# Scores' second products on 64 rows each, with a second copy of the rounded queries

## The chip, the cores and the metric

One core of a Trainium2 chip runs the program. The metric is the device time of one execution in microseconds (us). A row of matmul on TensorE is called PE, a load of its stationary operand (weights) PEld, VectorE is DVE, ScalarE is ACT, GpSimd is POOL, and the DMA queue of SyncE is SPq.

## What is computed

One encoder layer on two sequences (512 and 1024 tokens, width 1024). The change touches the scores of the attention heads:

```python
q = proj[..., :ATTN_WIDTH].reshape(B, S, N_Q_HEADS, HEAD_DIM)      # 8 heads of 64
k = proj[..., ATTN_WIDTH:ATTN_WIDTH + KV_WIDTH].reshape(B, S, N_KV_HEADS, HEAD_DIM)   # 2 heads of 64
...
s = jnp.einsum('bqkgd,bskd->bkgqs', qi, k, preferred_element_type=jnp.float32) * scale
p = jax.nn.softmax(s, axis=-1).astype(v.dtype)
return jnp.einsum('bkgqs,bskd->bqkgd', p, v)
```

Around it stand a norm, an input projection, a pooling mixer, an output projection and a squared-ReLU MLP of width 4096.

## The kernel before

Every matrix product keeps float32 accuracy with operands in a rounded format (fp32r). A value x is split into a high part (x rounded) and a low part (x minus the high part), and the products high x high, low x high and high x low are summed in PSUM.

**The scores.** A head is 64 deep and the array has 128 rows. So the tile `Qs` (line 126) holds, for each query block, the rounded queries on 64 partitions and their low parts on the other 64. `KA` holds the rounded keys on both halves of the partitions, `KB` the keys' low parts on both halves. One product of `Qs` with `KA` thus gives high x high plus low x high, and one of `Qs` with `KB` gives high x low plus low x low (line 1072). `scores(s, pair, idx, u)` makes one *unit*: two outputs of 128x512 (`h` = 0 and 1) in two neighbouring PSUM banks. For each `h` it issues the product with `KA` and then the one with `KB`. `s.n` is 0 for the short sequence (the prompt) and 1 for the long one (the sample). In a prompt unit the two outputs are two blocks of 128 queries against all 512 keys; in a sample unit they are one block of queries against the two halves of the keys.

**The jobs.** A job is 4 units. The prompt has 4 jobs (`pair` 0 to 3, two heads each), the sample 16 (`pair` 0 to 3, `idx` 0 to 3: one head of the pair and one half of its queries). A job has 8 turns `k`. In a turn TensorE transposes four 128x128 blocks of the exponentials `prob` two turns ahead (L1088) and multiplies the turn's transposed block by the values (`values`, L1103 with the high part `pThi`, L1104 with the low part `pTlo`). In every odd turn it also makes one unit of scores of a later job (`scored_in`): in turn 1 the last unit of the next job, in turns 3, 5 and 7 the first three of the job after it. Three PSUM banks hold the transposes, four the units, one the sum over the values.

**What the other engines do for a job.** ACT rounds each transposed block (`pThi`, L1339), makes the exponentials (L1424), and copies the result out (`o_full`). DVE subtracts (`pTlo`, L1837), takes the maxima of each unit (L1899), and for the sample copies value tiles for the next heads (`Vg`, L2022, two copies in four jobs). Between PE, ACT and DVE there are semaphores only: PE's `values` waits for `pTlo`, a unit of scores waits for the exponentials of the unit that had its banks (`exp_done`). The order on each engine is that of the code.

**The split of the queries.** For the prompt ACT rounds the queries (`split_q`, line 1400, eight calls, the last four of them beside the attention itself) and DVE or POOL makes the low parts. For the sample POOL does both (`split_q`, line 2506), three jobs ahead: rounding (L2516), then the low part (L2519). POOL also adds and scales the outputs (L2537, L2543) and computes the pooling windows.

The sample's pairs 0 to 2 are a loop (`Fori`) on PE, ACT and DVE; the last pair is written out.

Of the kernel before, what the change touches and what calls it, by code (L numbers as in the profile page):

```python
# [7 lines left out]
ALU = mybir.AluOpType  # L8
# [3 lines left out]
F32R = mybir.dt.float32r  # L12

P = 128
# [3 lines left out]
NQ, NKV = 8, 2  # L18
# [9 lines left out]
TT = T // P  # L28
# [23 lines left out]
def hybrid_layer(nc, x, g1, w_in, gqk, w_pool, pool_scale, w_out, g2, w_up, w_down,  # L52
                 ident_d, rope_d, edge_d, y):
    with ExitStack() as ctx:
        def sem(name):
            return ctx.enter_context(nc.semaphore(name))

        def at(name, off, shape, dt=F32):
            return nc.alloc_sbuf_tensor_at(name, [P] + shape, dt, offset=BASE + off)
# [42 lines left out]
        S = R + 43008  # L102
# [12 lines left out]
        KA = [at("KA0", X + 20480, [NKV, SEQ_P], F32R), at("KA1", S + 6144, [NKV, SEQ_S], F32R)]  # L115
        KB = [at("KB0", W, [NKV, SEQ_P], F32R), at("KB1", S + 14336, [NKV, SEQ_S], F32R)]
        Qs = at("Qs", W + 4096, [4, 512], F32R)
# [4 lines left out]
        o_full = at("o_full", S, [2, 512])  # L122
        o_part = at("o_part", S + 4096, [512])
        rinvb = at("rinvb", S + 32768, [512])
        rinvb_last = at("rinvb_last", R + 38912, [512])
        rinvd = nc.dram_tensor("rinvd", [3 * NQ, P, 4], F32).ap()
        sw_sample = [at(f"sw_sample{i}", S + 22528 + i * 4160, [SEQ_S + 2 * PAD]) for i in range(2)]
# [77 lines left out]
        ps = ctx.enter_context(nc.psum_tensor("ps", [P, 8, 512], F32))  # L205
# [29 lines left out]
        u_done = sem("u_done")  # L235
# [107 lines left out]
        FIRST = 1  # L343
# [45 lines left out]
        def pair_kv(pair):  # L389
            return pair // (NQ // 2 // NKV)  # L390
# [50 lines left out]
        def qk_cols(a, j, c0, n):  # L441
            return QT[a:a + 64, c0 // 32:(c0 + n) // 32, bass.ds(j, 1), :].rearrange("p b a t -> p b (a t)")

        def blocks(cols):
            return cols.rearrange("p (b t) -> p b t", t=32)
# [490 lines left out]
        def _(pe):  # L936
# [115 lines left out]
            def scores(s, pair, idx, u):  # L1052
                g = s.group(pair, idx, u)
                half = u // 2 if s.n == 0 else 0
                if u % (GRP // s.halves) == 0:
                    pe.wait_ge(q_lo[s.n], s.out(pair, idx, half) - NQ * s.n + 1)
                pe.wait_ge(k_dup[0], 32 + 32 * s.n)
                if s.n == 0:
                    pe.wait_ge(k_dup[1], 32)

                if not isinstance(g, int) or g >= 2:
                    pe.wait_ge(exp_done, g - 1)
                kv = pair_kv(pair)
                for h in range(2):

                    qt = u if s.n else 2 * (u % 2) + h
                    key0 = h * 512 * s.n
                    out = ps[:, 2 * (u % 2) + h]
                    q = Qs[:, 2 * s.parity(pair, idx) + half, qt * P:(qt + 1) * P]
                    pe.matmul(out, q, KA[s.n][:, bass.ds(kv, 1), key0:key0 + 512].rearrange("p a c -> p (a c)"),  # L1070
                              start=True, stop=False)
                    mm = pe.matmul(out, q, KB[s.n][:, bass.ds(kv, 1), key0:key0 + 512].rearrange("p a c -> p (a c)"),  # L1072
                                   start=False, stop=True)
                mm.then_inc(s_done, 1)

# [54 lines left out]
            def attend(s, pair, last=False):  # L1130
                for idx in range(s.per):
                    if s.n and idx == 3:
                        pe.wait_ge(k_dup[1], 64)
                    for k in range(STEPS):
                        if transposed_in(s, pair, idx, k) and not (s.n == 0 and pair == 0 and k == 0):
                            transpose_p(*transposed_in(s, pair, idx, k))


                        ends = (k + 1) % s.kts == 0
                        if ends:  # L1140
                            values(s, pair, idx, k)
                        if scored_in(s, pair, idx, k):
                            scores(*scored_in(s, pair, idx, k))
                        if not ends:
                            values(s, pair, idx, k)
                        if last and (idx, k) == (2, 3):
                            turn_wp()
                        if last and (idx, k) in FOLDS:
                            fold(FOLDS.index((idx, k)))

            def first_scores(u):

                if u == 0:

                    pe.wait_ge(qk_copied, FIRST + TT - 1)
                    pe.wait_ge(v_lo, FIRST + TT - 1)
                if u == 1:

                    pe.wait_ge(qk_copied, FIRST + TT)
                    pe.wait_ge(v_lo, FIRST + TT)  # L1160
                scores(seqs[0], 0, 0, u)
# [12 lines left out]
            project_block(NB - 1, True)  # L1174

            scores(seqs[0], 1, 0, 0)

            pe.wait_ge(u_saved, FIRST + TT // 2)
# [4 lines left out]
            scores(seqs[0], 1, 0, 2)  # L1183
            for pair in range(NQ // 2):
                attend(seqs[0], pair)
            with pe.Fori(0, NQ // 2 - 1) as pair:
                attend(seqs[1], pair)
            attend(seqs[1], NQ // 2 - 1, True)

# [142 lines left out]
        def _(act):  # L1332
# [5 lines left out]
            def copy(out, in_, **kw):  # L1338
                return act.activation(out, in_, ACT.Copy, **kw)  # L1339
# [59 lines left out]
            def split_q(s, pair, idx, unit):  # L1399

                j = s.job(pair, idx)
                act.wait_ge(qT_in[s.n], 16 * s.len // P)
                half = s.half_of(idx, unit * s.kts)
                a, c0 = half * 64, s.start + idx // 2 * 512

                if not isinstance(j, int) or j >= 2:
                    act.wait_ge(s_done, GRP * (j - 1))
                if isinstance(j, int) and j == 0 and unit == 0:

                    act.wait_ge(hT_lo, TT)  # L1410
                copy(blocks(Qs[a:a + 64, 2 * s.parity(pair, idx) + unit]), qk_cols(a, pair, c0, 512)).then_inc(q_hi, 1)

            def exps(s, pair, idx, u):
# [42 lines left out]
            def project_block(n, last):  # L1456
                for i in range(2 if n == 0 else 0, 4):
                    t = n * 4 + i
                    copy_qkv(t, qkv_banks(i))
                    square_qk(t)  # L1460
                    if t + 2 < TT:

                        act.wait_ge(u_done, FIRST + t // 2)
                        split_hT(t + 2, (i + 2) % 4)
                        square_x(t + 2)
                    if last and i == 1:

                        split_k(0, 0)
                        split_k(0, 1)
                        for pair in range(2):  # L1470
                            for unit in range(2):
                                split_q(seqs[0], pair, 0, unit)
                    if last and i == 3:

                        act.wait_ge(u_done, FIRST + TT // 2 - 1)
                        exps(seqs[0], 0, 0, 0)
                        exps(seqs[0], 0, 0, 1)
                    if last and i == 3:
                        exps(seqs[0], 0, 0, 2)
                        exps(seqs[0], 0, 0, 3)  # L1480
# [931 lines left out]
        def _(pool):  # L2412
# [93 lines left out]
            def split_q(s, pair, idx):  # L2506

                a, b = idx % 2 * 64, (1 - idx % 2) * 64
                c0, m = s.start + idx // 2 * 512, s.out(pair, idx, 0) - NQ + 1

                if done:
                    pool.wait_ge(win_step, done)
                pool.wait_ge(qT_in[s.n], 16 * s.len // P)
                pool.wait_ge(s_done, GRP * (s.job(pair, idx) - 1))
                pool.wait_ge(q_hi, NQ + m - 1)
                pool.tensor_scalar(blocks(Qs[a:a + 64, 2 * (idx % 2)]), qk_cols(a, pair, c0, 512), 1.0, 1.0, ALU.mult, ALU.mult  # L2516
                                   ).then_inc(q_hi, 1)
                pool.wait_ge(q_hi, NQ + m)
                pool.tensor_tensor(blocks(Qs[b:b + 64, 2 * (idx % 2)]), qk_cols(a, pair, c0, 512),  # L2519
                                   blocks(Qs[a:a + 64, 2 * (idx % 2)].bitcast(F32)), ALU.subtract).then_inc(q_lo[1], 1)  # L2520
                pool.wait_ge(q_lo[1], m)
# [67 lines left out]
            for s in seqs:  # L2589
                for pair in range(NQ // 2):  # L2590
                    for idx in range(s.per):
# [6 lines left out]
                        if nxt3 and nxt3[0].n:  # L2598
                            split_q(*nxt3)
# [155 lines left out]
```

## Time and profile before

| | |
|---|---|
| median of 3 runs | 1474.98 us (1473.99 to 1475.79) |
| profiled execution, its own time | 1475.89 us |
| its span in the trace | 1474.1 us |
| granted TensorE clock, mean | 0.999 |
| units of scores | 80 (16 prompt, 64 sample), 160 products with `KA`, 160 with `KB` |

The page gives the busy time of each engine, the span in 40 slices of 36.9 us, the chain of work that ended last and the costliest groups of instructions. A matmul's row has a modelled end: its duration is longer than the distance to the next matmul's start, so that the cost of a matmul is read from the distance of two starts.

### The profile page before, as it was taken

How to read it: one execution, taken by the hardware profiler on the slowest of the kernel's cores; microseconds unless marked ns; L12 is line 12 of the kernel's file. 1: busy time of each engine (PE TensorE's matmuls, PEld its weight loads, DVE VectorE, ACT ScalarE, POOL GpSimd, SP SyncE). 2: the span in 40 equal slices, each digit the busy share in tenths (PEclk: the TensorE clock that was granted, in tenths of full speed). 3: DMA queues.
4: the chain of work that ended last, by engine and by line, in shares of the span. 5: the costliest groups of instructions: out<-in, count | busy, mean ns of one | idle time of the engine just before them, and what ended most of it. 6: DMA issues, size and time to landing. Idle time of an engine off the chain costs nothing.

```text
span 1474.1 us, 23234 instructions
## 1 busy us (share of the span) xinstructions
PE 1463.4 (99%) x7812; PEld 1306.9 (89%) x7812; DVE 1055.7 (72%) x1254; ACT 729.1 (49%) x1251; POOL 398.1 (27%) x363
## 2 busy tenths in 40 slices
PE   9999999999999999999999999999999999999999
PEld 8999878888888889999999999999888888888887
DVE  6765799999868785544454454449887888878875
ACT  6232398888847755545555554546322322323220
POOL 3457567666745420000000000001220211311300
PEclk9999999999999999999999999999999999999999
DMA  8644341111245849333233334347644344343434
GB/s 263 149 119 118 82 126 34 40 25 24 81 164 192 292 154 380 128 144 141 103 143 133 136 114 151 121 174 278 253 157 158 100 157 126 117 155 109 138 97 183
DMA packets 94443, 212.30 MB, mean 144 GB/s; under 512 B 12080, under 2 KB 31408, under 8 KB 94256
## 3 DMA queue, kind: packets, MB, share of 16 engines
q1 hardware_dynamic: 92192, 200.46, 40.8%
q10 hardware_dynamic: 2192, 11.08, 1.8%
q8 instruction: 33, 0.54, 0.2%
q14 instruction: 26, 0.21, 0.1%
HBM read 133.08 MB, written 71.62 MB: 139 GB/s over the span
## 4 chain that ended last, share of the span: by engine, by line
PE 97%; ACT 1%; DVE 1%; issue 1%; DMA 0%; POOL 0%; ACTq 0%; SPq 0%; DVEq 0%; POOLq 0%
PE ps L943 24%; PE ps L944 24%; PE ps L945 24%; PE ps L1206 6%; PE ps L1088 4%; PE ps L1216 3%; PE ps L1103 2%; PE ps L1070 2%; PE ps L1104 2%; PE ps L1072 2%; ACT prob L1424 0%; DMA ident<-in_ident 0%; ACT pThi L1339 0%; PE ps L968 0%; PE ps L972 0%
## 5 line engine op out<-in xcount | busy, mean ns | idle before, releaser
L943 PE MATMUL ps<-h,wuhi 128*128 128x384 f32 (+1 forms) x904 | 301.5, 333 | 0.2 <-issue 0.2
L944 PE MATMUL ps<-h,wuhi 128*128 128x384 f32 (+1 forms) x904 | 301.1, 333 | 0.0
L945 PE MATMUL ps<-h,wulo 128*128 128x384 f32 (+1 forms) x904 | 301.1, 333 | 0.0
L943 PE MATMUL ps<-wdhi,hidhi 128*128 128x512 f32 x672 | 261.6, 389 | 0.0
L945 PE MATMUL ps<-wdhi,hidlo 128*128 128x512 f32 x672 | 261.5, 389 | 0.0
L944 PE MATMUL ps<-wdlo,hidhi 128*128 128x512 f32 x672 | 261.5, 389 | 0.0
L2328 DVE TENSOR_TENSOR yacc<-yacc,ps 128x1024 f32<-128x1024 f32 x167 | 203.1, 1216 | 78.8 <-PE ps L945 78.8
L1339 ACT ACTIVATE hidhi<-hin 128x1024 fp32r<-128x1024 f32 (+1 forms) x72 | 86.8, 1205 | 301.0 <-PE ps L945 291.8
L2242 DVE TENSOR_TENSOR u<-u,ps 128x384 f32<-128x384 f32 x96 | 53.0, 553 | 181.6 <-PE ps L945 181.6
L943 PEld LDWEIGHTS ps<-h,wuhi 128*128 128x128 f32 x904 | 169.7, 188 | 0.7 <-issue 0.4
L944 PEld LDWEIGHTS ps<-h,wuhi 128*128 128x128 f32 x904 | 169.7, 188 | 0.0
L945 PEld LDWEIGHTS ps<-h,wulo 128*128 128x128 f32 x904 | 169.7, 188 | 0.0
L943 PEld LDWEIGHTS ps<-wdhi,hidhi 128*128 128x128 f32 x672 | 126.1, 188 | 26.8 <-issue 0.4
L944 PEld LDWEIGHTS ps<-wdlo,hidhi 128*128 128x128 f32 x672 | 126.1, 188 | 26.1
L945 PEld LDWEIGHTS ps<-wdhi,hidlo 128*128 128x128 f32 x672 | 126.1, 188 | 26.1
L2684 POOL TENSOR_TENSOR hout<-h,hout 128x384 f32<-128x384 f32 x1 | 1.7, 1748 | 477.3 <-PE ps L945 477.3
L1837 DVE TENSOR_TENSOR pTlo<-ps,pThi 128x512 fp32r<-128x512 f32 x160 | 107.9, 686 | 12.4 <-ACT pThi L1339 9.6
L1837 DVE TENSOR_TENSOR hidlo<-hin,hidhi 128x1024 fp32r<-128x1024 f32 (+1 forms) x72 | 111.5, 1549 | 5.4 <-ACT hidhi L1339 5.4
L1643 ACT ACTIVATE hout<-u 128x384 f32<-128x384 f32 x96 | 50.4, 525 | 124.8 <-DVE u L2242 113.5
L1339 ACT ACTIVATE pThi<-ps 128x512 fp32r<-128x512 f32 x160 | 95.0, 601 | 26.4 <-PE ps L1088 19.7
L1088 PEld LDWEIGHTS ps<-ident,prob 128*128 128x128 f32 x640 | 79.3, 140 | 22.7 <-DVE pTlo L1837 1.4
L1424 ACT ACTIVATE prob<-ps,nmax 128x1024 f32<-128x1024 f32 (+1 forms) x96 | 93.0, 974 | 11.5 <-DVE nmax L1899 11.3
(229 smaller groups left out, 2813.8 us busy)
## 6 DMA issues: line engine op xcount, KB each, us to landing
hd<-hout SPq DMA_DIRECT2D x64, 384.0 KB, 3.2
hin<-hd SPq DMA_DIRECT2D x48, 512.0 KB, 3.6
hd<-hout SPq DMA_DIRECT2D x32, 576.0 KB, 2.8
hin<-hd SPq DMA_DIRECT2D x24, 768.0 KB, 4.4
wuraw<-in_w_up SPq DMA_DIRECT2D x17, 1024.0 KB, 5.9
wdraw<-in_w_down SPq DMA_DIRECT2D x8, 2048.0 KB, 9.3
h<-h2d ACTq DMA_DIRECT2D x7, 1536.0 KB, 10.8
x2in<-in_x SPq DMA_DIRECT2D x12, 512.0 KB, 3.3
```

The lines of the kernel that those rows point to most:

```text
L943: pe.matmul(out, w_hi, m_hi, start=start, stop=False, skip_group_check=resumed)
L944: pe.matmul(out, w_hi, m_lo, start=False, stop=False, skip_group_check=resumed)
L945: return pe.matmul(out, w_lo, m_hi, start=False, stop=stop, skip_group_check=resumed)
L1088: mm = pe.transpose(ps[:, 4 + k % 3, qt * P:(qt + 1) * P], prob[s.parity(pair, idx)][:, u, c0:c0 + P], ident[:])
L1206: pe.matmul(ps[:, 2 * i + h], c[i][:, k], wohi[:, j, h * 512:(h + 1) * 512], start=(j == 0 and c is chi), stop=False)
L1216: mm = pe.matmul(ps[:, 2 * i + h], chi[i][:, SLOT_ROWS[j]], wolo[:, j, h * 512:(h + 1) * 512], start=False, stop=(n == KT - 1))
L1339: return act.activation(out, in_, ACT.Copy, **kw)
L1424: ins = act.activation(prob[b][:, u, c0:c0 + s.len], psw[:, (u % 2) * 1024 + c0:(u % 2) * 1024 + c0 + s.len], ACT.Exp, bias=nmax[:, b, q:q ...
L1643: act.activation(out, src, ACT.Relu).then_inc(relu_done, 1)
L1837: return dve.tensor_tensor(out, a, b.bitcast(F32), ALU.subtract)
L2242: dve.tensor_tensor(u, u, up_bank(par, (1, 4, 5)[k]), ALU.add).then_inc(u_sum, 1)
L2328: dve.tensor_tensor(q, q, down_banks(u, o), ALU.add).then_inc(acc_done, 1)
```

## The change

The two products with `KA` come first, then the two with `KB`. For 72 of the 80 units (all but those of prompt pairs 0 and 1) each of the two products with `KB` uses only 64 rows: output 0 partitions 0 to 63, output 1 partitions 64 to 127, each with the rounded queries alone, so that the product low x low is no longer in the sum. The array is addressed as a tile of 64 rows for each of them (rows 0 to 63, rows 64 to 127). Since `Qs` has the rounded queries on one half of the partitions only, a new tile `Qh` holds them on the other half. ACT fills it for prompt pairs 2 and 3 (one more copy ahead of that of `Qs`, and a wait for the end of the input projection, whose weights lay there), POOL for every sample job. PE's loop over the sample's pairs 0 to 2 is written out (512 more matmuls in the program, as many as before executed).

```diff
+        Qh = at("Qh", S + 34816, [2, 512], F32R)
@@ scores
                 for h in range(2):
-                    q = Qs[:, 2 * s.parity(pair, idx) + half, qt * P:(qt + 1) * P]
-                    pe.matmul(out, q, KA[s.n][:, bass.ds(kv, 1), key0:key0 + 512].rearrange("p a c -> p (a c)"),
+                    c, keys, out = part(h)
+                    pe.matmul(out, Qs[:, 2 * slot + half, c], KA[s.n][:, bass.ds(kv, 1), keys].rearrange("p a c -> p (a c)"),
                               start=True, stop=False)
-                    mm = pe.matmul(out, q, KB[s.n][:, bass.ds(kv, 1), key0:key0 + 512].rearrange("p a c -> p (a c)"),
+                for h in range(2):
+                    c, keys, out = part(h)
+                    if s.n == 0 and pair < 2:
+                        r = slice(0, P)
+                    else:
+                        r = slice(h * 64, h * 64 + 64)
+                    q = Qh[r, slot, c] if r.stop - r.start == 64 and h != high else Qs[r, 2 * slot + half, c]
+                    mm = pe.matmul(out, q, KB[s.n][r, bass.ds(kv, 1), keys].rearrange("p a c -> p (a c)"),
                                    start=False, stop=True)
@@ TensorE's stream
-            with pe.Fori(0, NQ // 2 - 1) as pair:
+            for pair in range(NQ // 2 - 1):
                 attend(seqs[1], pair)
@@ ScalarE's split_q
+                if s.n == 0 and pair >= 2:
+                    act.wait_ge(u_done, FIRST + TT // 2)
+                    copy(blocks(Qh[64 - a:128 - a, s.parity(pair, idx)]), qk_cols(a, pair, c0, 512))
@@ GpSimd's split_q
+                pool.tensor_scalar(blocks(Qh[b:b + 64, idx % 2]), qk_cols(a, pair, c0, 512), 1.0, 1.0, ALU.mult, ALU.mult)
```

On PE, in the first job of the sample, turns 0 to 3, before (`prob_96` is the job's buffer of exponentials; the ISA and REGISTER_ALU rows are the loop's registers):

```order
L1088 MATMUL ps<-ident,prob_96 128x128 x4
L1062 ISA
L1070 ISA
L1070 MATMUL ps<-KA_92,Qs 128x512
L1072 REGISTER_ALU
L1072 MATMUL ps<-KB_94,Qs 128x512
L1070 ISA
L1070 MATMUL ps<-KA_92,Qs 128x512
L1072 REGISTER_ALU
L1072 MATMUL ps<-KB_94,Qs 128x512
L1101 REGISTER_ALU
L1103 MATMUL ps<-pThi,Vg 128x512
```

The same place now:

```order
L1099 MATMUL ps<-ident,prob_96 128x128 x4
L1074 MATMUL ps<-KA_92,Qs 128x512 x2
L1083 MATMUL ps<-KB_94,Qh 128x512
L1083 MATMUL ps<-KB_94,Qs 128x512
L1114 MATMUL ps<-pThi,Vg 128x512
L1115 MATMUL ps<-pTlo,Vg 128x512
```

The two products with the low parts are neighbours, between the two with the rounded keys and the values or the next transposes; the register instructions are gone.

On ACT, in the prompt's pair 0, where it rounds the queries of pairs 2 and 3, before:

```order
L1339 ACTIVATE pThi<-ps 128x512
L1339 ACTIVATE Qs<-QT 64x512
L1339 ACTIVATE pThi<-ps 128x512
L1424 ACTIVATE prob_96,rsum<-ps,nmax 128x512 x2
L1339 ACTIVATE Qs<-QT 64x512
L1339 ACTIVATE pThi<-ps 128x512 x2
```

The same place now:

```order
L1350 ACTIVATE pThi<-ps 128x512
L1350 ACTIVATE Qh<-QT 64x512
L1350 ACTIVATE Qs<-QT 64x512
L1350 ACTIVATE pThi<-ps 128x512
L1438 ACTIVATE prob_96,rsum<-ps,nmax 128x512 x2
L1350 ACTIVATE Qh<-QT 64x512
L1350 ACTIVATE Qs<-QT 64x512
L1350 ACTIVATE pThi<-ps 128x512 x2
```

Each copy into `Qs` has one into `Qh` ahead of it, and the next `pThi` comes behind both. POOL's stream has the same pattern, one `Qh` ahead of each `Qs` in the sixteen sample jobs.

## Rows read from the trace of the kernel before

**Rows 1.** The page, parts 1 and 2: busy time, granted clock in 40 slices.

```profile
PE 1463.4 (99%) x7812; PEld 1306.9 (89%) x7812; DVE 1055.7 (72%) x1254; ACT 729.1 (49%) x1251; POOL 398.1 (27%) x363
...
PEclk9999999999999999999999999999999999999999
```

**Rows 2.** Busy time by stretch: PE, PEld, DVE, ACT, POOL (instructions), clock, DMA.

```profile
190.00:217.00 27.00, 26.05 (x144) 20.43 (x144) 25.13 (x37) 25.73 (x63) 17.89 (x15) 1.00 0.40 114
217.00:237.00 20.00, 19.94 (x117) 16.48 (x116) 19.20 (x25) 18.14 (x37) 15.39 (x13) 1.00 0.23 48
240.00:393.00 153.00, 152.08 (x893) 127.48 (x891) 144.82 (x190) 133.51 (x237) 104.79 (x84) 1.00 0.13 28
```

**Rows 3.** DVE's waits from 240 to 393 us: total, times, longest.

```profile
DVE pTlo L1837 <- ACT pThi L1339: 5.1, 26, 0.2
```

**Rows 4.** Timeline of PE in sample jobs: start, duration, operation.

```profile
302.47 0.60 PE L1088 MATMUL ps<-ident,prob 128*128 128x128 f32 x4
302.82 0.48 PE L1070 MATMUL ps<-KA,Qs 128*128 x1
303.14 0.39 PE L1072 MATMUL ps<-KB,Qs 128*128 x1
303.14 0.19 PEld L1070 LDWEIGHTS ps<-KA,Qs 128*128 128x128 f32 x1
303.37 0.40 PE L1070 MATMUL ps<-KA,Qs 128*128 x1
...
303.60 0.40 PE L1072 MATMUL ps<-KB,Qs 128*128 x1
303.84 0.39 PE L1103 MATMUL ps<-pThi,Vg 128*128 128x512 f32 x1
...
304.65 0.48 PE L1103 MATMUL ps<-pThi,Vg 128*128 128x512 f32 x1
...
315.55 0.48 PE L1103 MATMUL ps<-pThi,Vg 128*128 128x512 f32 x1
```

**Rows 5.** Timeline of DVE in a stretch without idle time, prompt.

```profile
191.28 1.28 DVE L1837 TENSOR_TENSOR pTlo<-ps,pThi 128x512 fp32r<-128x512 f32 x2
192.47 0.17 DVE L1909 RECIPROCAL rinv<-rsum 128x4 f32<-128x4 f32 x1
...
193.13 1.21 DVE L1899 TENSOR_REDUCE nmax<-ps 128x2 f32<-128x1024 f32 x1
194.26 1.28 DVE L1837 TENSOR_TENSOR pTlo<-ps,pThi 128x512 fp32r<-128x512 f32 x2
```

**Rows 6.** Timeline of ACT around its roundings of the prompt's queries.

```profile
185.88 0.63 ACT L1339 ACTIVATE Qs<-QT 64x512 fp32r<-64x512 f32 x1
187.34 0.69 ACT L1424 ACTIVATE prob<-ps,nmax 128x512 f32<-128x512 f32 x1 [0.83 <-DVE nmax L1899]
...
199.67 0.63 ACT L1339 ACTIVATE Qs<-QT 64x512 fp32r<-64x512 f32 x1
200.19 1.07 ACT L1339 ACTIVATE pThi<-ps 128x512 fp32r<-128x512 f32 x2
...
204.05 0.63 ACT L1339 ACTIVATE Qs<-QT 64x512 fp32r<-64x512 f32 x1
204.70 0.69 ACT L1424 ACTIVATE prob<-ps,nmax 128x512 f32<-128x512 f32 x1
```

**Rows 7.** Timeline of POOL in a sample job.

```profile
303.93 1.29 POOL L2537 TENSOR_TENSOR attc<-o_full,o_part 64x512 f32<-64x512 f32 x1 [3.84 <-DMA o_part<-o_full]
...
306.95 0.61 POOL L2516 TENSOR_SCALAR Qs<-QT 64x512 fp32r<-64x512 f32 x1
```

**Rows 8.** Timeline where PE waits in the sample: DVE and PE.

```profile
365.46 2.32 DVE L2022 CAST Vg<-V 128x512 fp32r x1
...
368.52 0.47 PE L1103 MATMUL ps<-pThi,Vg 128*128 128x512 f32 x1 [0.92 <-DVE pTlo L1837]
```

More of the change, by code:

```diff
@@ L1063, in scores, with part @@
                 kv = pair_kv(pair)
-                for h in range(2):
-                    qt = u if s.n else 2 * (u % 2) + h
-                    key0 = h * 512 * s.n
-                    out = ps[:, 2 * (u % 2) + h]
-                    q = Qs[:, 2 * s.parity(pair, idx) + half, qt * P:(qt + 1) * P]
-                    pe.matmul(out, q, KA[s.n][:, bass.ds(kv, 1), key0:key0 + 512].rearrange("p a c -> p (a c)"),
-                              start=True, stop=False)
-                    mm = pe.matmul(out, q, KB[s.n][:, bass.ds(kv, 1), key0:key0 + 512].rearrange("p a c -> p (a c)"),
+                slot = s.parity(pair, idx)
+                high = idx % 2 if s.n else half
+                def part(h):
+                    qt = u if s.n else 2 * (u % 2) + h
+                    return slice(qt * P, (qt + 1) * P), slice(h * 512 * s.n, h * 512 * s.n + 512), ps[:, 2 * (u % 2) + h]
+                for h in range(2):
+                    c, keys, out = part(h)
+                    pe.matmul(out, Qs[:, 2 * slot + half, c], KA[s.n][:, bass.ds(kv, 1), keys].rearrange("p a c -> p (a c)"),
+                              start=True, stop=False)
+                for h in range(2):
[6 more added lines that the diff above has]
+                    mm = pe.matmul(out, q, KB[s.n][r, bass.ds(kv, 1), keys].rearrange("p a c -> p (a c)"),
                                    start=False, stop=True)
```

## The prediction

> **What bounds the kernel now.** I read the page first. TensorE is busy 99% of the span at the full granted clock [rows 1], so what an edit gives or costs on TensorE is the first question, and where another engine is nearly as full is the second. So I cut the attention into stretches [rows 2]. From 240 to 393 us (the sample jobs that still score) PE is busy 152.08 of 153 us, DVE 144.82 and ACT 133.51. There PE waits once, 0.92 us, behind a long `Vg` copy on DVE [rows 8]. DVE waits 5.1 us in all, in 26 short waits for ACT [rows 3], which itself follows PE's transposes. PE therefore sets the pace of the sample, with DVE some 5% behind it. From 190 to 217 us (prompt pairs 0 and 1) it is another picture: ACT is busy 25.73 of 27 us, more than DVE (25.13), and PE's modelled durations hide that it is not tight. From 217 to 237 us PE leads again (19.94 of 20), with ACT at 18.14 and DVE at 19.20.
>
> The timeline gives the unit costs [rows 4]. The start of one 128x512 product lies 0.23 us from the next (303.14, 303.37, 303.60, 303.84). The first product behind the transposes takes 0.32 (302.82 to 303.14), so a weight load that nothing hides costs about 0.09. Four transposes take 0.35. One job lasts 315.55 - 304.65 = 10.90 us.
>
> **The change part by part.**
>
> *The `KB` products.* A unit takes 4 x 0.23 = 0.92 us (1.01 behind transposes). If the two products on 64 rows run side by side, one 0.23 goes: that is the upper bound of the gain for a unit. If they run one behind the other, nothing goes. Against it stand two changes of the array's tiling in each unit, into 64 rows and back to 128, which the trace of before does not contain. Bounds for one of them from the nearest rows: nothing, if it is hidden like the steps at 303.37 and 303.60; 0.09 us if only a weight load comes to the open, as behind the transposes; 0.39 - 0.23 = 0.16 us if the next product has to wait for the modelled end of the last one; 0.16 + 0.09 = 0.25 us if both come together. So a unit changes by -0.23 + 2 x (0 to 0.25), from -0.23 to +0.27 us. The step behind the transposes is the nearest row, since it too is a change of what the array does. There it appears on one side only (the step into the transposes takes the usual 0.23), so I take 0.08 us in all for a unit and a net of -0.15 us.
>
> At this place the Trainium skill speaks on both sides. The page TensorEngine Tiling (Array Packing), section Tiling Modes, says that changing the tiling mode drains TensorE; by that rule each of the two changes costs at least the 0.16, a unit comes out 0.09 us longer, and the sum turns positive (the rival *full drain* below). The page TensorE: Matmul & The Clock Gate, Part 3, estimates the span of several row tiles as one matmul plus about 4 ns for each further tile, which gives the full 0.23 and says nothing of mixing them with full-height products. No row here can decide between them.
>
> *How many units count.* 57 units are scored inside sample jobs (the last of job 1, and four each of jobs 2 to 15), where PE leads: 57 x 0.15 = 8.6 us. DVE caps this. It has 153 - 144.82 = 8.2 us idle there [rows 2], and when its operations follow without idle time they overlap: the maxima take 1.13 instead of 1.21 (193.13 to 194.26), and two `pTlo` 1.19 instead of 1.28 [rows 5]. With 56 maxima this frees another 4.5 us, so DVE could follow by up to 12.7. The 8.6 fits, but the two `Vg` copies of each four jobs already push PE into a wait once, and with a faster PE they will do so more often. I take 7.5 of the 8.6.
>
> The other 15 tiled units are scored in the prompt. Eight or so lie before 217 us, where ACT is full: nothing. Seven lie in the stretch at 217 to 237 us: 7 x 0.15 = 1.1, of which half, since ACT and DVE have only 1.9 and 0.8 us of idle time there. That is 0.6.
>
> *ACT's four copies into `Qh`.* The first comes at 185.9, where ACT waits 0.83 us right behind (until 187.34) [rows 6]; one more copy at 0.55 is hidden, and the added wait for the end of the projection is past by then, since the maxima of the next unit wait for it as well. The other three lie in pair 0 and at the start of pair 1, where ACT is full. The step of such a copy is 0.52 (199.67 to 200.19) to 0.65 us (204.05 to 204.70); I take 0.55 each, 1.65 us, all on the path, because the next `pThi` and exponentials stand behind them and PE waits for those. Below it could be 0 if a later wait swallows it.
>
> *POOL's sixteen copies.* Each takes 0.61 us [rows 7]. In a sample job POOL waits 3.84 us for a DMA at the place shown, and it splits the queries of a job more than one job before PE asks for them. The cover is that lead; without it a job would lose 0.61. I take nothing.
>
> *The written-out loop.* PE has no idle time at the loop's turns now, so nothing is to be won; the register instructions sit between products that start 0.23 apart as anywhere. More program has to be fetched, as in the prompt, which is written out and shows no hole that recurs. I take nothing.
>
> **The sum.** -7.5 - 0.6 + 1.65 = -6.45 us against the profiled execution's 1475.89 (its span 1474.1, 1.8 around it), so 1469.4. That execution lies 0.9 above the median of the runs; against 1474.98 the forecast is **1468.5 us**.
>
> **The rivals.** 0.2% of this time is 2.95 us, about what a measurement can tell from no change.
>
> - *Side by side and cheap* (the forecast; a unit gains 0.12 to 0.23 us): 1463 to 1471 us. For it: weight loads start together with the product before them, on the same 128 rows (the load and the product at 303.14 [rows 4]), so loads for a 64-row tile should be hidden too. Chance 0.40.
> - *The changes of tiling eat the gain* (0.09 each, a unit gains 0.05): 57 x 0.05 = 2.9, less 1.65, so 1473.7; with the neighbouring values 1472 to 1477. Chance 0.19.
> - *Full drain, slower.* The place is each unit's two borders. The point from which it decides is 0.11 us for one change of tiling, above which a unit gets longer. At 0.16 each it costs 0.09 x 72 = 6.5, and with ACT's 1.65, less what is hidden in the prompt, 1482; at 0.25 each it costs 0.27 x 57 = 15.4, some 2 in the prompt and 1.65, so 1494. For it: a modelled duration of 0.39 against 0.23 shows work still in the array when the next product starts, and a change of its shape may have to wait for that. Against it: the transposes are a change of mode too and cost 0.09 only. Chance 0.29, of which 0.10 beyond 1488.
> - *No overlap at all* (two 64-row products one behind the other, no price for the change): only ACT's copies are left, 1476.6. Chance 0.05.
> - *DVE becomes the bound at once*: its waits for ACT (5.1 us) turn out to be latency that stays, so that it gives back only 3 of 8.2 us: 1475 - 3 + 1.65 = 1473.6. Chance 0.07.
>
> **How the numbers follow.** Faster by over 0.2%: the first case and a little of the second, 0.43. Within 0.2%: most of the second, the fourth and the fifth, 0.27. Slower: 0.30. The range 1462 to 1488 leaves out only the heavy drain; the forecast's own range is 1463 to 1471.
>
> **What the profile after would show.** If right, the second of the two `KB` products starts less than 0.1 us behind the first, the `KA` product before and the values behind it start at 0.23 to 0.3 us, and a sample job takes about 10.3 us instead of 10.90, with DVE close to full. Pairs 0 and 1 are longer by 1 to 2 us, from ACT. If the drain rules, the first `KB` product starts 0.35 us or more behind the `KA` one, and what stands behind the second too, with a job above 10.9. If the starts of the two `KB` products lie 0.23 apart, they do not overlap. What would make the prediction wrong is above all the price of the two changes of tiling, which enters 57 times.

## The result, and the profile after

The changed kernel takes **1485.78 us** (median of 6 runs, 1485.21 to 1487.92) against 1474.80 of the kernel before on the same chip (6 runs, 1473.99 to 1475.79): ratio 1.008, 95% interval 1.007 to 1.009. It is slower by 11.0 us. The forecast was 1468.5. What came is the rival *full drain*. One run in all is left out of a median here, one of e10, which took 2341.02 us at a mean clock of 0.567.

The page of the changed kernel, parts 1 and 2 (beside [rows 1]):

```profile
PE 1473.1 (99%) x7812; PEld 1286.3 (87%) x7812; DVE 1059.3 (71%) x1254; ACT 732.0 (49%) x1255; POOL 407.6 (27%) x379
...
PEclk9999999999999999999999999999999999999999
```

The same number of matmuls at the same clock keeps PE busy for 9.7 us longer (1463.4 before), although pairs of them now run at the same time. The clock is out of the question.

Busy time by stretch of the changed kernel (columns as in [rows 2]):

```profile
190.00:217.00 27.00, 24.75 (x131) 16.12 (x130) 23.18 (x35) 25.53 (x60) 16.26 (x15) 1.00 0.40 104
217.00:237.00 20.00, 20.00 (x112) 14.20 (x112) 18.74 (x25) 17.48 (x36) 16.16 (x15) 1.00 0.23 48
240.00:393.00 153.00, 152.19 (x846) 106.74 (x845) 138.90 (x179) 126.25 (x225) 105.17 (x92) 1.00 0.13 28
```

From 240 to 393 us PE is as busy as before, but gets through 846 matmuls instead of 893, 5% fewer. DVE does 179 operations instead of 190, and is busy 138.90 us instead of 144.82. So PE still sets the pace, and it is a slower pace. From 190 to 217 us ACT is the full engine, as before.

The timeline of PE in the sample jobs, as [rows 4] (start, duration, operation; a row with x2 or x4 holds that many neighbours):

```profile
301.81 0.60 PE L1099 MATMUL ps<-ident,prob 128*128 128x128 f32 x4
302.17 0.70 PE L1074 MATMUL ps<-KA,Qs 128*128 128x512 f32 x2
302.80 0.49 PE L1083 MATMUL ps<-KB,Qh 64*128 64x512 f32 x1
302.80 0.49 PE L1083 MATMUL ps<-KB,Qs 64*128 64x512 f32 x1
303.22 0.50 PE L1114 MATMUL ps<-pThi,Vg 128*128 128x512 f32 x1
303.56 0.39 PE L1115 MATMUL ps<-pTlo,Vg 128*128 128x512 f32 x1
...
304.15 0.48 PE L1114 MATMUL ps<-pThi,Vg 128*128 128x512 f32 x1
...
315.66 0.47 PE L1114 MATMUL ps<-pThi,Vg 128*128 128x512 f32 x1
```

The two `KB` products have the same start, 302.80: they run side by side, and one step of 0.23 us is gone. Around them every step is longer. From the first `KA` product to the first `KB` one it is 0.63, where 0.32 (behind the transposes) and 0.23 would be 0.55: +0.08. From the pair to the values it is 0.42 instead of 0.23: +0.19. From the first product of the values to the second it is 0.34 instead of 0.23: +0.11. Together that is 0.38 us for the two changes of tiling. The stretch from the first `KA` product to the second product of the values is 303.56 - 302.17 = 1.39 us, against 304.06 - 302.82 = 1.24 before: +0.15 a unit, which is 0.38 - 0.23. The job takes 315.66 - 304.15 = 11.51 us instead of 10.90: +0.61, four units of 0.153.

The weight loads of the same place, PEld:

```profile
302.14 0.30 PEld L1074 LDWEIGHTS ps<-KA,Qs 128*128 128x128 f32 x2
302.79 0.18 PEld L1083 LDWEIGHTS ps<-KB,Qh 64*128 64x128 f32 x1 [0.35 <-issue]
302.80 0.18 PEld L1083 LDWEIGHTS ps<-KB,Qs 64*128 64x128 f32 x1
303.22 0.19 PEld L1114 LDWEIGHTS ps<-pThi,Vg 128*128 128x128 f32 x1 [0.24 <-issue]
```

Before, a load started together with the product before its own (303.14 in [rows 4]). Here the first load after each change starts together with its own product: nothing was fetched across the change. The load path is idle ahead of it, and no semaphore is named, only "issue". In the list of waits from 240 to 393 us PEld has these entries (total us, times, longest), where before it had one, 1.1 us, once, at L1103:

```profile
PEld ps L1083 <- issue: 18.8, 52, 0.4
PEld ps L1114 <- issue: 7.3, 27, 1.0
PEld ps L1099 <- issue: 3.2, 13, 0.2
PEld ps L1114 <- DVE pTlo L1851: 3.2, 13, 0.2
```

The 52 at L1083 are the changes into 64 rows. The others are the 52 changes back, each with 0.24 or 0.25 us: 26 + 13 ahead of the values, 13 ahead of the next transposes (the 27th at L1114, 1.0 us, is the wait behind the long `Vg` copy, as before). For 13 of them DVE is named, at the same length.

**Where the 11 us lie.** I take three marks: the prompt's first product with the values, the sample's first one, and the transposes of `wp_raw`, which PE makes in the sample's last job but one (394.50 us before, 404.57 now). The first two bound "the prompt's stretch", the last two "the sample's". Against the experiment with 128-row products and all copies (e2 below), the prompt's stretch is 49.55 instead of 48.49 us, +1.06, which is the seven tiled units that lie there where PE leads (7 x 0.153 = 1.07). The sample's is 166.72 us against 158.03 before, +8.7: 57 units of 0.153. ACT's copies add 1.8 (e2). That is 11.6 us, for 11.0 measured.

Against e2 the sample's stretch is longer still, 166.72 instead of 157.04, +9.7. The 1.0 above the 57 units lies in a single job, which takes 12.59 us where its neighbours take 11.52. The kernel before has such a job too (12.07 instead of 10.90), and e2 has none. It holds the long `Vg` copy on DVE of [rows 8], for which PE waits 0.81 us in the changed kernel (the last section).

### The profile page after: what moved, and what is told of

Read it like the earlier page. It is cut to its first block, busy times and chain, and to the rows that moved or that the text cites. A ratio compares the mean times of both kernels' runs of the same rounds, so it can differ in the third digit from the quotient of the medians.

```text
span 1484.2 us, 23088 instructions
## 1 busy us (share of the span) xinstructions
PE 1473.1 (99%) x7812; PEld 1286.3 (87%) x7812; DVE 1059.3 (71%) x1254; ACT 732.0 (49%) x1255; POOL 407.6 (27%) x379
## 4 chain that ended last, share of the span: by engine, by line
PE 89%; POOL 4%; issue 2%; ACT 2%; DVE 2%; DMA 0%; ACTq 0%; POOLq 0%; SPq 0%; DVEq 0%
PE ps L944 22%; PE ps L945 22%; PE ps L946 22%; PE ps L1217 6%; PE ps L1099 4%; PE ps L1227 3%; PE ps L1114 3%; PE ps L1115 2%; PE ps L1074 2%; PE ps L1083 2%; POOL rsqk L2440 1%; POOL qsin L2499 1%; POOL sw_prompt L2469 1%; ACT prob L1438 1%; DVE roped L1957 0%
## 5 line engine op out<-in xcount | busy, mean ns | idle before, releaser
L1099 PE MATMUL ps<-ident,prob 128*128 128x128 f32 x640 | 97.1, 274 | 1.1 <-DVE pTlo L1851 0.9
```

The lines of the kernel that those rows point to most:

```text
L1099: mm = pe.transpose(ps[:, 4 + k % 3, qt * P:(qt + 1) * P], prob[s.parity(pair, idx)][:, u, c0:c0 + P], ident[:])
```

## The experiments

In all of them the kernel before ran on the same chip beside the new one. "Step" is the distance between two starts.

### e1_order: the order and the written-out loop alone

The whole change without the 64-row tiles and without `Qh`: the two `KA` products first, 128 rows everywhere.

```diff
-                    if s.n == 0 and pair < 2:
+                    if True:
                         r = slice(0, P)
...
-                    copy(blocks(Qh[64 - a:128 - a, s.parity(pair, idx)]), qk_cols(a, pair, c0, 512))
...
-                pool.tensor_scalar(blocks(Qh[b:b + 64, idx % 2]), qk_cols(a, pair, c0, 512), 1.0, 1.0, ALU.mult, ALU.mult)
```

> The changed kernel with all products on 128 rows and without the copies into Qh: what is left of the change is the order of the four products of a unit and the written-out loop. If the price is the array's change of tiling: no change from before, 1474 to 1476.5 us. If the written-out loop or the order costs: up to the 1486 of the changed kernel.

Measured: 1474.56 us against 1474.43, ratio 0.9999 (0.9990 to 1.0008). Order and loop cost nothing, as the prediction took.

### e2_copies: the copies without the tiles

e1 with ACT's four and POOL's sixteen copies back: only the `if True:` above.

> As the run with order and loop alone, but with ACT's four and POOL's sixteen copies into Qh, which nothing reads. If the tiling is the price: the 1.65 us of the prediction for ACT's copies, so 1475.5 to 1477.5. If the copies are the cause (ACT full in the prompt, POOL late in the sample): 1483 to 1486.

Measured: 1475.02 us, ratio 1.0006 (0.9997 to 1.0015), just below the expected 1475.5 to 1477.5. In the whole time the copies cannot be told from nothing. In the trace they can: the prompt's stretch is 48.49 us instead of 46.72 in e1, +1.77. PE waits for ACT there, in the timeline of PE in e2:

```profile
201.11 0.50 PE L1114 MATMUL ps<-pThi,V 128*128 128x512 f32 x1 [0.91 <-ACT o_full L1350]
```

The changed kernel's timeline has the same wait:

```profile
201.45 0.50 PE L1114 MATMUL ps<-pThi,V 128*128 128x512 f32 x1 [0.79 <-ACT o_full L1350]
```

The sample's stretch, though, is 157.04 us instead of 158.55: 1.5 us come back. They lie in two of its jobs: the one with the long copy takes 10.90 us instead of 12.07, and the first 11.06 instead of 11.41 (the last section has the cause).

### e3_same_tile: both products on rows 0 to 63

The same work, the same two changes of tiling, but no chance to run side by side. Output 1 takes the queries and keys of the lower half here.

```diff
-                        r = slice(h * 64, h * 64 + 64)
-                    q = Qh[r, slot, c] if r.stop - r.start == 64 and h != high else Qs[r, 2 * slot + half, c]
+                        r = slice(0, 64)
+                    q = Qh[r, slot, c] if r.stop - r.start == 64 and high else Qs[r, 2 * slot + half, c]
```

> The changed kernel with both products with KB on rows 0 to 63, so that they can't run side by side; the changes of tiling are as many as in the changed kernel. If the two products do overlap now and the borders are the price: 0.23 us more for each of 72 units, of which 57 on the path, so 1498 to 1503. If they gain nothing from being side by side: 1486.

Measured: 1500.85 us against 1474.43, ratio 1.0179 (1.0163 to 1.0194), 15 us above the changed kernel and inside the expected 1498 to 1503. Without the overlap a unit costs 0.39 more than before (0.153 + 0.24; a sample job takes 12.43 us), and 64 x 0.39 + 1.8 = 26.8 us for the 26.4 measured. The timeline of PE in e3:

```profile
302.87 0.73 PE L1083 MATMUL ps<-KB,Qs 64*128 64x512 f32 x2
303.53 0.50 PE L1114 MATMUL ps<-pThi,Vg 128*128 128x512 f32 x1
303.87 0.39 PE L1115 MATMUL ps<-pTlo,Vg 128*128 128x512 f32 x1
```

From the first `KB` product to the values it takes 0.66 us, in the changed kernel 0.42. The overlap is real and worth 0.24. The step behind it is 0.34 in both. So the pair does what it should, and the loss is around it.

### e4_kb_first: the pair next to the transposes

The `KB` pair ahead of the two `KA` products. If the price were the weight load in the open, which the transposes leave there anyway, the two could share it.

```diff
                 for h in range(2):
-                    pe.matmul(out, Qs[:, 2 * slot + half, c], KA[s.n][:, bass.ds(kv, 1), keys].rearrange("p a c -> p (a c)"),
-                              start=True, stop=False)
+                    pe.matmul(out, q, KB[s.n][r, bass.ds(kv, 1), keys].rearrange("p a c -> p (a c)"),
+                                   start=True, stop=False)
                 for h in range(2):
-                    mm = pe.matmul(out, q, KB[s.n][r, bass.ds(kv, 1), keys].rearrange("p a c -> p (a c)"),
-                                   start=False, stop=True)
+                    mm = pe.matmul(out, Qs[:, 2 * slot + half, c], KA[s.n][:, bass.ds(kv, 1), keys].rearrange("p a c -> p (a c)"),
+                              start=False, stop=True)
```

> The changed kernel with the two 64-row products ahead of the two with KA in each unit, so that the step into 64 rows stands behind the transposes in three of four units, where a weight load is in the open anyway. If the price of a border is in part that load: up to 0.09 us less in 43 units, 1481 to 1484. If it is a drain that comes whatever stands ahead: 1485 to 1487.

Measured: 1486.65 us against 1474.43, ratio 1.0089 (1.0075 to 1.0103): as slow as the changed kernel. The expected 1481 to 1484 of a shared load did not come, and the other outcome did, 1485 to 1487. The timeline of PE:

```profile
302.13 0.60 PE L1099 MATMUL ps<-ident,prob 128*128 128x128 f32 x4
302.66 0.50 PE L1079 MATMUL ps<-KB,Qh 64*128 64x512 f32 x1
302.66 0.50 PE L1079 MATMUL ps<-KB,Qs 64*128 64x512 f32 x1
303.09 0.73 PE L1083 MATMUL ps<-KA,Qs 128*128 128x512 f32 x2
303.66 0.40 PE L1114 MATMUL ps<-pThi,Vg 128*128 128x512 f32 x1
```

The transposes now take 0.53 us to the next start instead of 0.35, the pair 0.43, and the first `KA` product 0.34 (303.66 less the usual 0.23 lies 0.34 behind 303.09). It is the same price in other places: from the transposes to the values 303.66 - 302.13 = 1.53 us, against 303.84 - 302.47 = 1.37 before, +0.16 a unit.

### e5_half and e6_sample: fewer units

e5 tiles prompt pairs 2 and 3 and every second unit of the sample; e6 tiles the sample alone and has no copies on ACT.

```diff
-                    if s.n == 0 and pair < 2:
+                    if s.n == 0 and pair < 2 or s.n and u % 2:
```

```diff
-                    if s.n == 0 and pair < 2:
+                    if s.n == 0:
...
-                    copy(blocks(Qh[64 - a:128 - a, s.parity(pair, idx)]), qk_cols(a, pair, c0, 512))
```

> The changed kernel with 64-row products only in the sample units with even u (32 of 64), and in the prompt as changed. The price goes by units: a job of the changed kernel is 0.61 us longer for four units, so 0.15 for each; 29 fewer such units on the path take back about 4.4 us of the 11.4, 1480 to 1482. If a fixed part (copies, program) carried it: 1484 or more.

> The changed kernel with 64-row products in the sample alone, and without ACT's copies: 64 units tiled. If the sample's units carry the loss (57 x 0.15 = 8.7, and up to 1 for the seven scored late in the prompt): 1483 to 1485. If the prompt's part with ACT's copies is large (2 us or more): 1482 or less.

Measured: e5 1479.64 us against 1473.56, ratio 1.0045 (1.0031 to 1.0059), +6.1, just below the expected 1480 to 1482; e6 1484.96, ratio 1.0078 (1.0064 to 1.0092), +11.4, inside the expected 1483 to 1485. The loss grows with the number of tiled units of the sample: none in e2, 32 in e5, 64 in e6. A sample job of four units takes 10.90 us with none tiled, 11.20 with two (e5) and 11.52 with four (e6). In e6 the sample's stretch is 166.72 us, as in the changed kernel. The whole loss of e6 is 1.6 us above 64 x 0.153 = 9.8. The two stretches account for 10.3 of it (48.02 and 166.72 us, against 46.42 and 158.03 before), and I have no cause for the rest; differences of 1 us between such variants are not resolved by this sum.

### e7_twice and e8_four: the price by itself

e7 makes the `KB` pair twice in a row (so the low parts are counted twice, in the two prompt pairs at 128 rows as well): twice the work on 64 rows, still two changes. e8 goes back to the order `KA`, `KB`, `KA`, `KB` with `KB` on 64 rows: the same work as the changed kernel, four changes, no pair.

```diff
+                    pe.matmul(out, q, KB[s.n][r, bass.ds(kv, 1), keys].rearrange("p a c -> p (a c)"),
+                                   start=False, stop=False)
+                for h in range(2):
...
                     mm = pe.matmul(out, q, KB[s.n][r, bass.ds(kv, 1), keys].rearrange("p a c -> p (a c)"),
                                    start=False, stop=True)
```

```diff
                               start=True, stop=False)
-                for h in range(2):
-                    c, keys, out = part(h)
                     if s.n == 0 and pair < 2:
```

> The changed kernel with the pair of 64-row products made twice in each unit (the prompt pairs 0 and 1 make the full-height ones twice), so the keys' low parts count double. The changes of tiling stay as many. If only the borders are dear and a second pair inside costs one product's step: 0.23 us for 80 units, 65 to 80 of them on the path, 1500 to 1505. If each pair inside 64 rows also costs a weight load in the open (0.32): 1507 to 1512.

> The changed kernel with the four products of a unit in the order of before (KA, KB, KA, KB), the KB ones on 64 rows: four changes of tiling in a unit where there were two, and no two products side by side. With 0.20 us for a change: 4 x 0.20 = 0.80 for each of 72 units, 57 or more on the path, 1520 to 1533. If what costs is something once per unit: 0.23 more than the changed kernel, 1499 to 1503.

Measured: e7 1504.27 us against 1473.56, ratio 1.0208 (1.0193 to 1.0224); e8 1529.05, ratio 1.0374 (1.0358 to 1.0390), +55.5 us, of which 64 x 0.79 + 1.8 = 52.4 come out of the steps below. Both are inside what was expected of a price per change (1500 to 1505, 1520 to 1533). The timeline of PE in e7:

```profile
293.32 0.49 PE L1083 MATMUL ps<-KB,Qh 64*128 64x512 f32 x1
...
293.65 0.39 PE L1092 MATMUL ps<-KB,Qh 64*128 64x512 f32 x1
293.65 0.39 PE L1092 MATMUL ps<-KB,Qs 64*128 64x512 f32 x1
293.98 0.50 PE L1123 MATMUL ps<-pThi,Vg 128*128 128x512 f32 x1
```

From the first pair to the values it is now 0.33 + 0.33 = 0.66 instead of 0.42: a second pair costs 0.24, the price of one ordinary product. The price is per change and not per product. And in e8:

```profile
292.08 0.48 PE L1074 MATMUL ps<-KA,Qs 128*128 128x512 f32 x1
292.49 0.49 PE L1081 MATMUL ps<-KB,Qh 64*128 64x512 f32 x1
292.91 0.50 PE L1074 MATMUL ps<-KA,Qs 128*128 128x512 f32 x1
293.34 0.50 PE L1081 MATMUL ps<-KB,Qs 64*128 64x512 f32 x1
293.77 0.50 PE L1112 MATMUL ps<-pThi,Vg 128*128 128x512 f32 x1
294.11 0.39 PE L1113 MATMUL ps<-pTlo,Vg 128*128 128x512 f32 x1
```

The five steps are 0.41, 0.42, 0.43, 0.43 and 0.34, together 2.03 us. With 128 rows they were 0.32 + 4 x 0.23 = 1.24. Four changes cost 0.79, 0.20 each; a sample job takes 14.02 us instead of 10.90. The steps can also be read as one price in two parts. The first step has only the change ahead of it: 0.41 - 0.32 = 0.09. The last has only the change behind it: 0.34 - 0.23 = 0.11. Those in the middle have both: 0.42 to 0.43 - 0.23 = 0.19 to 0.20. So a change of tiling delays its own product by 0.09 and the next one by 0.11 us. The same two numbers give the steps of e7, 0.23 + 0.11 behind the first pair and 0.23 + 0.09 ahead of the values, for 0.33 and 0.33 measured. The loads of e8:

```profile
292.49 0.18 PEld L1081 LDWEIGHTS ps<-KB,Qh 64*128 64x128 f32 x1 [0.24 <-issue]
292.91 0.19 PEld L1074 LDWEIGHTS ps<-KA,Qs 128*128 128x128 f32 x1 [0.24 <-issue]
293.34 0.18 PEld L1081 LDWEIGHTS ps<-KB,Qs 64*128 64x128 f32 x1 [0.24 <-issue]
```

Each load stands at the start of its own product, with the load path idle ahead of it for 0.24 us and no semaphore named.

### e9_all64: two pairs for one visit

The `KA` products go on 64 rows too, with the rounded queries alone, so the product of the low queries with the rounded keys is left out in the 72 units. Four products on 64 rows then follow each other.

```diff
-                    pe.matmul(out, Qs[:, 2 * slot + half, c], KA[s.n][:, bass.ds(kv, 1), keys].rearrange("p a c -> p (a c)"),
-                              start=True, stop=False)
...
+                    pe.matmul(out, q, KA[s.n][r, bass.ds(kv, 1), keys].rearrange("p a c -> p (a c)"),
+                                   start=True, stop=False)
```

> The changed kernel with the products with KA on 64 rows too, with the rounded queries alone; it leaves out the product of the queries' low parts with the rounded keys in 72 units. A unit is now two pairs side by side between the same two changes of tiling. If those two cost 0.40 us and each pair saves 0.23: 0.46 - 0.40, so 0.06 less than before for each of 57 units and more, 1470 to 1473. If products on 64 rows are slow in themselves: not below the changed kernel's 1485.

Measured: 1471.69 us against 1474.62, ratio 0.9981 (0.9972 to 0.9990), inside the expected 1470 to 1473. Its timeline of PE:

```profile
290.00 0.60 PE L1104 MATMUL ps<-ident,prob 128*128 128x128 f32 x4
290.53 0.50 PE L1079 MATMUL ps<-KA,Qs 64*128 64x512 f32 x1
...
290.87 0.39 PE L1088 MATMUL ps<-KB,Qs 64*128 64x512 f32 x1
...
291.20 0.50 PE L1119 MATMUL ps<-pThi,Vg 128*128 128x512 f32 x1
291.53 0.40 PE L1120 MATMUL ps<-pTlo,Vg 128*128 128x512 f32 x1
```

From the transposes to the second product of the values it is 1.53 us, against 304.06 - 302.47 = 1.59 before: two pairs save 0.46 and two changes cost 0.40. In the whole time this stands beside ACT's copies and the long copy, which is missing here as in e2. Against e2, which has the same copies, the sample's stretch is 153.33 instead of 157.04 us: 57 x 0.065.

### e10_no_low: how far DVE lets PE run

e1 without any `KB` product: the low parts of the keys are left out everywhere. It asks what a much cheaper unit could have brought at most.

```diff
-                    pe.matmul(out, Qs[:, 2 * slot + half, c], KA[s.n][:, bass.ds(kv, 1), keys].rearrange("p a c -> p (a c)"),
-                              start=True, stop=False)
-                for h in range(2):
...
-                    mm = pe.matmul(out, q, KB[s.n][r, bass.ds(kv, 1), keys].rearrange("p a c -> p (a c)"),
-                                   start=False, stop=True)
+                    mm = pe.matmul(out, Qs[:, 2 * slot + half, c], KA[s.n][:, bass.ds(kv, 1), keys].rearrange("p a c -> p (a c)"),
+                              start=True, stop=True)
```

> The kernel with order and loop alone, without any product with KB (the keys' low parts are left out of the scores): TensorE has 0.46 us less in each unit, 1.84 in a job of 10.90. It asks how much a faster TensorE could give at all. If DVE and ACT cap it at 8.2 to 12.7 us of idle time as in the prediction: 1460 to 1467. If they follow with TensorE: 14 jobs x 1.84 = 26 less, 1446 to 1450.

Measured: 1459.87 us against 1474.62, ratio 0.9896 (0.9878 to 0.9914), -14.75 us, at the edge of the expected 1460 to 1467. By PE's steps 0.46 x 57 = 26 us would have gone in the sample alone. Its busy time from 240 to 380 us, columns as in [rows 2]:

```profile
240.00:380.00 140.00, 134.73 (x785) 106.20 (x783) 136.28 (x189) 129.52 (x238) 103.28 (x82) 1.00 0.15 31
```

From the list of PE's waits in the same stretch (total, times, longest):

```profile
PE ps L1090 <- DVE pTlo L1839: 3.0, 14, 0.3
```

DVE is now the fullest engine, at 136.28 of 140 us, and PE waits for its `pTlo` ahead of the transposes in 14 places. Its shortest jobs take 9.8 us, where 10.90 less PE's 1.84 would be 9.06.

### e11_pool: the version to keep

128-row products in the new order, POOL's copies kept, ACT's taken out (e2 showed that these cost 1.8 us in the prompt while something gave 1.5 back in the sample).

```diff
-                    if s.n == 0 and pair < 2:
+                    if True:
...
-                    copy(blocks(Qh[64 - a:128 - a, s.parity(pair, idx)]), qk_cols(a, pair, c0, 512))
```

> All products on 128 rows, order and loop of the changed kernel, POOL's sixteen copies into Qh kept, ACT's four left out. The trace with all the copies was 1.8 us longer in the prompt than the one without any, and 1.5 us shorter in the sample, where the last long Vg copy on DVE took 0.50 us instead of 2.31. If ACT's copies made the first and POOL's shift the second: about 1.5 us less than order and loop alone, 1472.5 to 1473.8, with no Vg copy over 2 us and the prompt stretch (first product with the values to the sample's first) back at 46.7 us. If the two belong together: 1474 to 1475.5.

Measured: 1472.78 us (11 runs) against 1474.27 (15 runs), ratio 0.9989 (0.9980 to 0.9998): 1.5 us faster than the kernel before, and some 13 us faster than the changed one, each set against the runs of before on its own chip (1.008 - 0.9989 = 0.0091 of 1474). The prompt's stretch is 46.67 us, the sample's 156.88.

## Why the prediction was wrong

**The step that failed** is the price of the two changes of tiling: "I take 0.08 us in all for a unit and a net of -0.15 us". It is 0.38 to 0.40 in all (changed kernel, e8), and the net is +0.15. The bounds held: 0.20 for one change lies between 0.16 and 0.25, the two that had the next product wait for the last one. The choice between them was wrong. I went by the nearest row, the step behind the transposes at 0.32. e8 shows how little of the price that row has: it is as large as one of the two parts of a change (0.09, beside 0.09 and 0.11), and it comes on one border only. The step into the transposes costs nothing above the usual 0.23; the step into 64 rows costs 0.09 and leaves 0.11 to the next. What was at hand against the row was the prediction's own argument for the drain, that a modelled 0.39 us of work is in the array when the next product starts after 0.23.

The rule that the prediction weighed, from the Trainium skill's page TensorEngine Tiling (Array Packing), section Tiling Modes, that a change of mode drains TensorE, is what the steps of e8 look like, at 0.20 us each where the prediction put at least 0.16 beside it. That the array really empties in the first 0.09 us, and that the held-back load makes the other 0.11, is read from the loads' starts and not shown by a run of its own.

**Side by side.** Right: both `KB` products start at 302.80, and e3 gives 0.24 us for the overlap, where 0.23 was the bound. The Trainium skill's page TensorE: Matmul & The Clock Gate, Part 3, agrees with this part; the mixing that it doesn't speak of is where the loss is.

**The number of units.** Right: 57 x 0.153 = 8.7 us is what the sample's stretch grew by against before (both with one job of the long copy), and 7 x 0.153 = 1.07 what the prompt's did (1.06). The eight units ahead of 217 us cost nothing, where ACT is full (in the table of stretches PE has 2.25 us idle there).

**ACT's copies.** Right in place and nearly in size: 1.65 foreseen for three of them, 1.77 in e2's prompt stretch. In the timeline of ACT in the changed kernel the two copies are 0.64 and 0.65 us apart from what follows, where 0.55 was put:

```profile
203.72 0.63 ACT L1350 ACTIVATE Qh<-QT 64x512 fp32r<-64x512 f32 x1
204.36 0.63 ACT L1350 ACTIVATE Qs<-QT 64x512 fp32r<-64x512 f32 x1
205.01 0.69 ACT L1438 ACTIVATE prob<-ps,nmax 128x512 f32<-128x512 f32 x1
```

**POOL's copies, the order, the loop.** Nothing was foreseen, and e1 shows nothing for the last two. POOL's copies cost nothing either; they moved POOL's work, and the wait behind the long `Vg` copy went with it in e2 and e11, which I had not thought of.

**DVE's cap.** It was put at 8.2 to 12.7 us in the sample. The change never came to it, since PE got slower. e10 brings it out: the whole kernel gains 14.75 us where PE's steps would give over 26. The sample's stretch is 145.30 us instead of 158.03, 12.7 less, of which over 1 us is the job with the long copy (9.90 us there). So the cap is real, and lies near the upper of the two numbers.

**The rival.** *Full drain* had its point of decision at 0.11 us for one change, and 1482 at 0.16 and 1494 at 0.25. In the unit's own terms, 0.153 x 57 = 8.7, with seven units and ACT's copies on top 11.6, gives 1486.4 from 1474.8; 1485.8 was measured.

## What to carry to other kernels

Each change between 128-row and 64-row tiles cost about 0.20 us here, at the full clock, with one pair, two pairs or a single product between the changes; a pair of 512-column products side by side saves 0.23, so a visit with one pair loses 0.15 to 0.17 and one with two gains about 0.06 (one visit for the pairs of two units wasn't tried). Where a price has no row in the trace, the row that looks nearest may hold only a part of it: ask of each border of the new state what is in flight there, and put both bounds into the sum before choosing, above all where the term enters 57 times. A step that engages once a unit is worth one run that multiplies it (e7, e8) before the kernel is rewritten around it.

## What the runs showed of the hardware that I had not expected

**A change of tiling has two parts**, 0.09 us ahead of its product and 0.11 behind it, at the full clock. The weight load for the new tile starts with its own product (292.49 in e8), though the loads within 128-row tiling start with the product before (303.14 in [rows 4]). Transposes next to the change share nothing of its price (e4).

**A DVE copy takes 0.4 or 2.3 us by what POOL is doing.** The copies `Vg` go from SBUF to SBUF. With no POOL operation beside it one takes 0.42 us, in the timeline of DVE before:

```profile
321.84 0.42 DVE L2022 CAST Vg<-V 128x512 fp32r x1
```

The slowest one in e1, with the POOL operation beside it:

```profile
363.61 2.41 POOL L2479 TENSOR_TENSOR up<-sw_sample,up 128x1024 f32<-128x1024 f32 x1
363.99 2.31 DVE L2033 CAST Vg<-V 128x512 fp32r x1
```

The same copy in e11:

```profile
364.55 0.51 DVE L2033 CAST Vg<-V 128x512 fp32r x1
...
364.86 2.45 POOL L2479 TENSOR_TENSOR up<-sw_sample,up 128x1024 f32<-128x1024 f32 x1
```

In e1 the copy starts behind the POOL operation and ends 0.28 us after it (366.30, 366.02). So does the one in [rows 8], behind which PE waits 0.92 us, and every longer `Vg` copy in the traces of before, the changed kernel, e1, e2, e5, e6 and e11 that starts behind a POOL `TENSOR_TENSOR` still running: it ends 0.28 to 0.30 us after that one, so that it takes from 0.43 to 2.49 us. In e11 it starts ahead of the long POOL operation, just before the end of a shorter one (364.78), and takes 0.51. The other side pays in e5, where the copy starts at 369.13 and the POOL operation 0.03 us behind it:

```profile
369.16 2.64 POOL L2482 TENSOR_TENSOR up<-sw_sample,up 128x1024 f32<-128x1024 f32 x1
```

That is 0.2 us more than its usual 2.4. The Trainium skill's page SBUF — State Buffer, section SBUF: two separate sides, says that DVE and GpSimd have a pair of ports in common, which whichever starts first holds for its whole instruction; of DVE's operations it names those in a 2-port performance mode and those with two SBUF inputs. The copy has one input, and no trace shows its mode, but the rows agree with the rule: the loser pays up to 1.9 us for a copy of 0.4.

The copies into `Qh` moved POOL's work by some tenths of a microsecond, so that in e2 and e11 this pair meets the other way round, and the sample's stretch is 157.04 and 156.88 us there instead of 158.03 and 158.55. In the changed kernel they meet as before (the copy takes 2.49 us from 373.95). For e11 against before the place is shown: the job with the long copy takes 10.91 us instead of 12.07, which is the whole difference of the two stretches. That it is also the 1.5 us of the whole time fits but isn't shown: no run moved POOL's operation alone, and the lower end of that gain is only 0.02%.
